# Other start addresses in SBUF for the float32r operands of the matmuls in a transformer and Hyena/MLA layer, one core

## What is computed

```python
# first block
x = x + 0.5 * rmsnorm(swiglu(rmsnorm(x) , w_gu, w_down))          # ffn1, 1024 -> 2*2816 -> 1024
q, k, v, z, xbc, dt, gates = split(rmsnorm(x) @ w_in)             # 10272 columns
attn_out = rmsnorm(diff_attention(q, k, v)) @ w_branch_attn
ssd_out = rmsnorm(ssd(silu(conv(xbc)), dt) * silu(z)) @ w_branch_ssd
x = x + rmsnorm((g_attn * attn_out + g_ssd * ssd_out) @ w_mix_out)
x = x + rmsnorm(attention(rmsnorm(x) @ xa_w_q, rmsnorm(mem) @ xa_w_kv) @ xa_w_o)
x = x + 0.5 * rmsnorm(swiglu(rmsnorm(x), w_gu, w_down))           # ffn2
# second block
hy_in, z_hy, c_q, c_kv, k_rope, z_attn, gates = split(rms_norm(x) @ w_in_2)
u_hy = (long_conv(hy_in) * silu(z_hy)) @ w_hy_out
u_attn = (mla_attention(c_q, c_kv, k_rope) * silu(z_attn)) @ w_attn_out
x = x + (g_hy * u_hy + g_attn * u_attn) @ w_out
```

## Time and profile before

| | us |
|---|---|
| median of the runs (1118.72 to 1119.15, 2 runs) | 1118.93 |
| the profiled execution's own time | 1118.72 |
| its span, first to last instruction | 1116.9 |
| TensorE matmul busy | 1101.3 (99%) |
| TensorE weight load busy | 1042.9 (93%) |
| VectorE busy | 792.8 (71%) |
| ScalarE busy | 590.6 (53%) |

### The profile page before, as it was taken

The page is one execution under the profiler, slowest core; times in us unless marked ns, Lnnn a source line. Parts: engine busy times, 40 slices in busy tenths (PEclk is TensorE's granted clock), DMA queues, the critical chain, the costliest instruction groups (busy, mean ns, idle before and its releaser), DMA issues.

```text
span 1116.9 us, 20894 instructions
## 1 busy us (share of the span) xinstructions
PE 1101.3 (99%) x8484; PEld 1042.9 (93%) x8484; DVE 792.8 (71%) x1112; ACT 590.6 (53%) x844; POOL 0.2 (0%) x4
## 2 busy tenths in 40 slices
PE   9999999999999999999999999999999999999998
PEld 7999999999999999999999898999999799999998
DVE  5765555858898967777777867665555686987774
ACT  5443444557764335687644655444444566564561
POOL 0000000000000000000000000000000000000000
PEclk9999999999999999999999999999999999999999
DMA  8665555455444335444555434455555346443341
GB/s 298 242 223 188 192 183 189 171 192 181 175 156 147 102 129 204 155 148 151 189 177 179 166 114 160 133 209 204 181 179 204 123 162 216 163 151 114 114 151 38
DMA packets 29137, 188.59 MB, mean 169 GB/s; under 512 B 3496, under 2 KB 4809, under 8 KB 7370
## 3 DMA queue, kind: packets, MB, share of 16 engines
q1 hardware_dynamic: 26592, 181.42, 46.7%
q10 hardware_dynamic: 2474, 6.15, 1.7%
HBM read 186.50 MB, written 1.05 MB: 168 GB/s over the span
## 4 chain that ended last, share of the span: by engine, by line
PE 83%; DVE 12%; ACT 3%; issue 1%; DMA 1%; SPq 0%; DVEq 0%; ACTq 0%
PE bank L515 25%; PE bank L517 24%; PE bank L516 24%; DVE sb_w_lo L1988 3%; PE bank L596 2%; DVE sb_ssd_conv L2211 2%; PE bank L831 1%; ACT sb_w_hi L1302 1%; PE bank L976 1%; PE bank L670 1%; DMA sb_w_raw<-in_w 1%; PE bank L1048 0%; PE bank L1184 0%; PE bank L1027 0%; PE bank L1207 0%
## 5 line engine op out<-in xcount | busy, mean ns | idle before, releaser
L1988 DVE TENSOR_TENSOR sb_w_lo<-sb_w_raw,sb_w_hi 128x2048 fp32r<-128x2048 f32 x169 | 386.5, 2289 | 156.1 <-ACT sb_w_hi L1302 155.9
L515 PE MATMUL bank<-sb_hT_hi,sb_w_hi 128*128 128x256 f32 x1560 | 444.4, 285 | 1.2 <-DVE sb_hT_lo L2065 1.2
L516 PE MATMUL bank<-sb_hT_lo,sb_w_hi 128*128 128x256 f32 x1560 | 437.8, 281 | 0.0
L517 PE MATMUL bank<-sb_hT_hi,sb_w_lo 128*128 128x256 f32 x1560 | 436.9, 280 | 0.0
L1302 ACT ACTIVATE sb_w_hi<-sb_w_raw 128x2048 fp32r<-128x2048 f32 x169 | 322.5, 1908 | 36.1 <-PE bank L517 34.7
L515 PEld LDWEIGHTS bank<-sb_hT_hi,sb_w_hi 128*128 128x128 f32 x1560 | 293.3, 188 | 5.9 <-issue 4.0
L516 PEld LDWEIGHTS bank<-sb_hT_lo,sb_w_hi 128*128 128x128 f32 x1560 | 293.7, 188 | 2.3 <-issue 1.2
L517 PEld LDWEIGHTS bank<-sb_hT_hi,sb_w_lo 128*128 128x128 f32 x1560 | 295.0, 189 | 0.1
L1356 ACT ACTIVATE sb_ffn_gate<-sb_ffn_gate 128x256 f32<-128x256 f32 x44 | 18.4, 418 | 140.4 <-DVE sb_ffn_gate L2080 140.4
L515 PE MATMUL bank<-sb_w_hi,sb_hT_hi 128*128 128x256 f32 x256 | 73.3, 286 | 1.0 <-DVE sb_w_lo L1988 0.7
L516 PE MATMUL bank<-sb_w_lo,sb_hT_hi 128*128 128x256 f32 x256 | 71.4, 279 | 0.0
(11 more groups left out here) (431 smaller groups left out, 1748.8 us busy)
## 6 DMA issues: line engine op xcount, KB each, us to landing
sb_w_raw<-in_w SPq DMA_DIRECT2D x169, 1024.0 KB, 5.0
sb_x<-in_x SPq DMA_DIRECT2D x2, 512.0 KB, 4.4
sb_w_raw<-in_w SPq DMA_DIRECT2D x4, 256.0 KB, 7.0
sb_w_raw<-in_w SPq DMA_DIRECT2D x2, 512.0 KB, 8.2
sb_mem_xn<-in_mem ACTq DMA_DIRECT2D x1, 1024.0 KB, 8.3
sb_post_g<-in_ffn_post_g ACTq DMA_DIRECT2D x2, 512.0 KB, 5.3
sb_decay<-in_c_decay ACTq DMA_DIRECT2D x1, 768.0 KB, 4.3
out<-sb_x SPq DMA_DIRECT2D x3, 256.0 KB, 2.1
```

The lines of the kernel that those rows point to most:

```text
L515: pe.matmul(o, a_hi, b_hi, start=first, stop=False)
L516: pe.matmul(o, a_hi, b_lo, start=False, stop=False)
L517: return pe.matmul(o, a_lo, b_hi, start=False, stop=last)
L1988: tt(w_lo[b % STAGES][:], w_raw[b % RING][:], f32(w_hi[b % STAGES][:]), ALU.subtract).then_inc(w_lo_in, 1)
```

## The change

Eight lines of start addresses are given other numbers. `FFN_AT` becomes a number for each ffn, and the room behind the two `hT` tiles is written as the largest entry of `X_AT` (64 elements, as before), so every other tile keeps its address. The instructions, their order on each engine and their semaphores are the same one for one; only the addresses in them differ.

```diff
-FFN_AT = 64
-
-X_ROOM = 64
-
-X_AT = {"ffn1": 16, "mix": 48, "y": 18, "xa": 14, "ffn2": 48, "sec": 50, "fin": 46}
+FFN_AT = {1: 96, 2: 224}
+
+X_AT = {"ffn1": 32, "mix": 24, "y": 8, "xa": 40, "ffn2": 64, "sec": 12, "fin": 20}
...
-        hT_hi = begins_at(sb("hT_hi", [P, KD * SEQ + X_ROOM], F32R))
+        hT_hi = begins_at(sb("hT_hi", [P, KD * SEQ + max(X_AT.values())], F32R))
...
-                "hi": place(24 + FFN_AT * BYTE, f"ffn{n}_hi", [P, 2, SEQ], F32R),
-                "lo": place(26 + FFN_AT * BYTE, f"ffn{n}_lo", [P, 2, SEQ], F32R),
+                "hi": place(24 + FFN_AT[n] * BYTE, f"ffn{n}_hi", [P, 2, SEQ], F32R),
+                "lo": place(26 + FFN_AT[n] * BYTE, f"ffn{n}_lo", [P, 2, SEQ], F32R),
...
-        mem_hi = place(82 + 128 * BYTE, "mem_hi", [P, KD, SEQ], F32R)
+        mem_hi = place(82 + 96 * BYTE, "mem_hi", [P, KD, SEQ], F32R)
...
-        mixed_hi = place(16, "mixed_hi", [P, KD, SEQ], F32R)
+        mixed_hi = place(16 + 128 * BYTE, "mixed_hi", [P, KD, SEQ], F32R)
...
-        xa_hi = place(32 - 384 * BYTE, "xa_hi", [P, KD, SEQ], F32R)
+        xa_hi = place(32 - 256 * BYTE, "xa_hi", [P, KD, SEQ], F32R)
...
-        sec_hi = place(8 + 128 * BYTE, "sec_hi", [P, KD, SEQ], F32R)
+        sec_hi = place(8 + 288 * BYTE, "sec_hi", [P, KD, SEQ], F32R)
...
-        cq_hi = place(39, "cq_hi", [P, 3, SEQ], F32R)
+        cq_hi = place(39 - 128 * BYTE, "cq_hi", [P, 3, SEQ], F32R)
```

More of the change, by code:

```diff
@@ L287, in program @@
         post_eps = sb("post_eps", [P, TOK])
-        hT_lo = begins_at(sb("hT_lo", [P, KD * SEQ + X_ROOM], F32R))
+        hT_lo = begins_at(sb("hT_lo", [P, KD * SEQ + max(X_AT.values())], F32R))
         square = sb("square", [P, 6 * P])
@@ L334, in program @@
         mem_junk = place(68, "mem_junk", [P, 1, D])
-        mem_hi = place(82 + 128 * BYTE, "mem_hi", [P, KD, SEQ], F32R)
-        mem_lo = place(90 + 128 * BYTE, "mem_lo", [P, KD, SEQ], F32R)
+        mem_hi = place(82 + 96 * BYTE, "mem_hi", [P, KD, SEQ], F32R)
+        mem_lo = place(90 + 96 * BYTE, "mem_lo", [P, KD, SEQ], F32R)
         xa_k = place(0, "xa_k", [P, KD, SEQ])
@@ L386, in program @@
         mg = place(48, "mg", [P, KD, SEQ])
-        mixed_hi = place(16, "mixed_hi", [P, KD, SEQ], F32R)
-        mixed_lo = place(24, "mixed_lo", [P, KD, SEQ], F32R)
+        mixed_hi = place(16 + 128 * BYTE, "mixed_hi", [P, KD, SEQ], F32R)
+        mixed_lo = place(24 + 128 * BYTE, "mixed_lo", [P, KD, SEQ], F32R)
         xa_q = place(16, "xa_q", [P, KD, SEQ])
@@ L395, in program @@
         xa_st = place(30, "xa_st", [P, 4, 2])
-        xa_hi = place(32 - 384 * BYTE, "xa_hi", [P, KD, SEQ], F32R)
-        xa_lo = place(40 - 384 * BYTE, "xa_lo", [P, KD, SEQ], F32R)
+        xa_hi = place(32 - 256 * BYTE, "xa_hi", [P, KD, SEQ], F32R)
+        xa_lo = place(40 - 256 * BYTE, "xa_lo", [P, KD, SEQ], F32R)
         post_tmp = place(56, "post_tmp", [P, 512])
@@ L419, in program @@
         sec_xn = place(24, "sec_xn", [P, TOK, D])
-        sec_hi = place(8 + 128 * BYTE, "sec_hi", [P, KD, SEQ], F32R)
-        sec_lo = place(48 + 128 * BYTE, "sec_lo", [P, KD, SEQ], F32R)
+        sec_hi = place(8 + 288 * BYTE, "sec_hi", [P, KD, SEQ], F32R)
+        sec_lo = place(48 + 288 * BYTE, "sec_lo", [P, KD, SEQ], F32R)
         mv = place(24, "mv", [P, TOK, MLA_HEADS, V_DIM])
@@ L427, in program @@
         c_junk = place(37, "c_junk", [P, Q_LORA])
-        cq_hi = place(39, "cq_hi", [P, 3, SEQ], F32R)
-        cq_lo = place(42, "cq_lo", [P, 3, SEQ], F32R)
-        ckv_hi = place(45, "ckv_hi", [P, 2, SEQ], F32R)
-        ckv_lo = place(47, "ckv_lo", [P, 2, SEQ], F32R)
+        cq_hi = place(39 - 128 * BYTE, "cq_hi", [P, 3, SEQ], F32R)
+        cq_lo = place(42 - 128 * BYTE, "cq_lo", [P, 3, SEQ], F32R)
+        ckv_hi = place(45 - 128 * BYTE, "ckv_hi", [P, 2, SEQ], F32R)
+        ckv_lo = place(47 - 128 * BYTE, "ckv_lo", [P, 2, SEQ], F32R)
         hyF = place(32, "hyF", [P, 12, SEQ])
```

## The result

The changed kernel took 1130.86 us (median of two runs, 1130.61 and 1131.10) against 1118.93 before: a ratio of 1.0106, 95% interval 1.0063 to 1.0150. It is slower by about 12 us, and the forecast was a gain of 6. The profiled execution took 1131.03 us with a span of 1129.2.

The account below looks back on a forecast made before the run. The prediction took the distances between TensorE's back-to-back matmuls to bound the kernel. From 1118.72 us it took 6.0 for part (a) and 0 for (b) and (c), giving 1112.7, stated as 1113 us, range 1100 to 1126.

Parts of the forecast that it names:

- What bounds the kernel: TensorE is busy 1101.3 of 1116.9 us, so time changes only if matmuls come closer together or further apart.
- The classes: Operands sorted by offset from a multiple of 64 bytes: aligned outside the ffns 115.3 ns on average, 8 above 120, 8 below 117.8.
- part (c): ffn1 and ffn2 up, mixed and xa_hi move to another multiple of 64 bytes: 0, bounds -9.5 and +1.4 us.
- Part (b): mix, mem, sec_hi and the ffns' down product move from a multiple of 64 bytes to 32 above one: 0 us.
- Part (a): sec, y, xa and fin move from 8 bytes off to multiples of 16, reaching 115.3 ns: -6.0 us, bounds -9.0 and +0.8.
- Rival 2: Half a line is worse than 8 bytes: operands moved to 32 bytes go to 120 ns, 1132 us; mild or full, chance 0.16.
- Rival 3: The pace level is an accident of breaks, the address does nothing: 1118.7 +- 1.5 us; chance 0.19, shared with cancelling gains and losses.

Follow-up runs that it names:

- e7: The kernel before with mix, y, xa and fin at byte 0 and sec, ffn1, ffn2 at byte 128; 1129.73 us, one execution.
- e9: The kernel before with w_hi, w_lo, w_raw, x and both hT tiles 64 bytes further on, sec's view at 192; 1123.07 us, one execution.
- e4: The kernel before with only sec moved to byte 48 and y to byte 32; 1119.23 us, ratio 0.9998.
- e8: The kernel before with y, xa, sec and fin at byte 192, mix at 72, ffn hi and lo halves 64 bytes further on; 1125.59 us, one execution.
- e10: The kernel before with all streamed hT views at byte 192, fin left at 184; 1118.80 us, ratio 0.9997.
- e1: The changed kernel with the mix stage's hT halves back at byte 192; 1125.77 us, ratio to before 1.0055.
- e3: The changed kernel with the hT views of ffn1 and ffn2 back at bytes 64 and 192; 1123.65 us, ratio to before 1.0034.
- e12: e10 with the ffn hi and lo halves of both ffns 160 bytes further on; 1114.75 us, ratio to before 0.9961.
- e16: The kernel before with ffn1, ffn2 and xa at byte 112, mix and y at 192, sec at 48, fin at 64; 1111.10 us, ratio 0.9926.
- e17: e16 with sec at byte 112 instead of 48; 1111.55 us, ratio to before 0.9922.
- e13: The kernel before with every streamed hT view at byte 112 and fin at 64; 1113.86 us, ratio 0.9955.

## Why the prediction was wrong

- *What bounds the kernel*: right. TensorE's distances carry the 12.3 us, and no engine beside it changed.
- *The classes*: this step failed. The prediction sorted operands by the distance to a multiple of 64 bytes. All 229 runs that it called aligned stood 64 above a multiple of 128, and the trace could not tell the two readings apart. e7 and e9 show that for 256 columns the period is 128 bytes, and the reference the other operand. In part (c), the move to another multiple of 64 was costed at 0 with +1.4 us as its worst; the ffn up views moved from the best class (64) to the worst (0), and that is 1004 x 0.9 + 1047 x 2.5 ns = 3.5 us. `mixed` gave 0.9 more, but e4 shows that this needs no move.
- *Part (b)*, costed at 0 with bounds -5.3 and +12.4, came to about +10 us in distances, of which 1.5 were won back in breaks: mix at 96 was near its upper end of 8.4 (5.4 us in the streamed and 1.0 in the stationary part), mem 0.9. The down product lost 2.9 us, twice its own upper bound of 1.5: the ckv row gave 229.5 ns, and 233.3 was there to be had. This term was mis-sized.
- *Part (a)*, costed at -6.0: the four stages gained 1.4 (sec), 0.6 (y) and 0.0 (xa) us in distances and lost 0.4 in fin. The value 115.3 for them was the mean of a class that they did not enter; e8 and e10, which put them into it, show 114.5 to 115.6 ns. And the stage sec cannot turn most of it into time: the prediction asked only whether the weights would come fast enough, and not about the softmax chain. The slow matmuls hid that chain: TensorE waits 0.4 us for it at 120.1 ns, 1.1 to 1.2 at 118.4 and 2.5 to 3.1 at 114.1 to 115.3.
- *Rival 2* gave 1132 us and is the one that came true in place, mix above all. That its total is within 1.2 us of the measured one is luck: it had mix at +8.4, which took 4.8 us more, the down product at +1.5 (2.9), (a) at +0.8 (about -0.4 in the stages), and nothing for the ffns' up product (3.5) or `mixed` (0.9). Its mechanism, that half a line is worse than 8 bytes, holds at byte 96 only, where mix has 120 ns; at byte 32 it has 116.7.
- *Rival 3*, an accident of breaks: wrong as a whole, since one number brought mix back in e1. It is right inside a class: at distance 64 both paces occur, and what ran before (e3, e12) and the single execution (mem in e4) have a say in it.
- *The range* began at 1100 and ended at 1126, 5 us short. It left out the upper half of rival 2, and part (c) had room for a loss of 1.4 us only.

## What to carry to other kernels

When a kernel is bound by back-to-back matmuls, read the distance between starts, not busy time or length, and look at the address of both operands: here one number in a table was worth 5 us, and the best table that was tried (e16) beats both kernels: 1111.10 us, 0.9926 of the kernel before, timed beside it. Sort what you see by several periods before you name one; where all samples of the trace share a residue, the trace cannot tell. And before a stage's matmuls are made faster, look for the chain that its slow matmuls hide: the gain can turn into a wait, and, as the windows of e17 show, a lower clock can come behind the wait.

## What was not expected of the hardware

Distances between float32r matmuls of 256 columns, with 128 stationary columns loaded for each, by the distance modulo 128 bytes from the stationary weights to the streamed operand:

| distance, bytes | 0 | 16 | 32 | 48 | 56 | 64 | 72 | 80 | 96 | 112 |
|---|---|---|---|---|---|---|---|---|---|---|
| ns, mean of a stage | 118.6-120.0 | 117.5-118.4 | 116.7-118.7 | 118.3-118.4 | 118.2-118.4 | 113.3-117.8 | 120.1-121.1 | 119.1 | 119.7-119.9 | 113.8-116.1 |

At 64 single runs have 113.3 or 117.8 ns, and those at 117.8 keep it until a break; at 112 nearly all end at 113.3 (the 116.1 is y in e13, whose blocks alternate with y2, so that nearly every run begins slower and settles). When the activation is the stationary operand, 64 is again the only class that reaches 113.3 (mix, fin), and 112 costs 120.0. With 512 columns and weights at multiples of 1,024, the stationary halves at 32, 64 and 160 bytes above a multiple of 1,024 cost 232.9 to 233.4 ns, at 128 232.4, and at 0 226.8 to 228.7; the distance modulo 128 does not sort these (e8 against e9). Most distances were tried in one or two stages only, and that the period is 128 and no multiple of it is shown best for 0 (bytes 0, 128 and 256) and 64 (bytes 64 and 192). What in a break picks the pace, and why these distances, was not tried and stays open.
